# Expert lists of a routed MLP: odd experts filled from the other end, the eleventh weight chunk in two halves, the first two freed places refilled in quarters

## The reference

```python
g_prob = softmax(hf @ w_route_group + b_route_group)           # 4 groups, the best one is taken
e_logits = (hf @ w_route_expert + b_route_expert)[..., group]  # 8 experts in it, the best two are taken
comb = g_w * softmax(top_l)
out[token] += silu(x @ w_gate[e]) * (x @ w_up[e]) @ w_down[e] * comb     # for both experts e of each token
```

## Time and profile before

| | |
|---|---|
| median of 3 runs | 1010.31 us (1009.67 to 1010.51) |
| the profiled execution's own time | 1011.65 us |
| its span (first to last instruction) | 1009.7 us |
| mean granted TensorE clock | 0.965 |
| moved by DMA | 258.53 MB |

### The profile page before, as it was taken

The page is one execution under the profiler, slowest core; times in us unless marked ns, Lnnn a source line. Parts: engine busy times, 40 slices in busy tenths (PEclk is TensorE's granted clock), DMA queues, the critical chain, the costliest instruction groups (busy, mean ns, idle before and its releaser), DMA issues.

```text
span 1009.7 us, 11128 instructions
## 1 busy us (share of the span) xinstructions
PE 881.6 (87%) x4299; PEld 484.0 (48%) x4299; DVE 374.1 (37%) x827; ACT 218.3 (22%) x559; POOL 94.2 (9%) x104
## 2 busy tenths in 40 slices
PE   6999999999999999999799997768787777777674
PEld 4555777777688888654443332222222222222221
DVE  4589687786353445522742111011111110111110
ACT  3432645446332100121111111001010110101010
POOL 0100000000000000011011220101010101111011
PEclk9999999999999999999879999999898999899998
DMA  9621321121122227298389999999999999999991
GB/s 319 208 84 67 101 83 51 43 84 42 42 84 84 84 111 275 80 422 340 128 296 393 387 392 387 400 401 404 396 399 404 408 395 408 405 409 405 404 380 37
DMA packets 34916, 258.53 MB, mean 256 GB/s; under 512 B 9304, under 2 KB 12632, under 8 KB 19608
## 3 DMA queue, kind: packets, MB, share of 16 engines
q1 hardware_dynamic: 27904, 242.17, 60.6%
q0 software_dynamic: 6960, 15.65, 5.5%
HBM read 252.45 MB, written 14.58 MB: 264 GB/s over the span
## 4 chain that ended last, share of the span: by engine, by line
PE 77%; issue 7%; DMA 7%; DVE 4%; another core or an unknown queue 2%; ACT 1%; SPq 1%; POOL 0%; POOLq 0%; DVEq 0%; ACTq 0%
PE ps L1785 24%; PE ps L2069 20%; PE ps L2092 12%; PE ps L1723 6%; PE ps L1944 5%; DMA arena<-in_w_gu 5%; DMA arena<-in_x 2%; PE ps L2054 1%; PE ps L1870 1%; PE ps L1844 1%; PE ps L1801 1%; PE ps L1827 1%; PE ps L1978 1%; PE ps L2077 1%
## 5 line engine op out<-in xcount | busy, mean ns | idle before, releaser
L1785 PE MATMUL ps<-arena 128*128 128x272 f32 x1120 | 266.7, 394 | 2.7 <-DVE arena L1283 1.0
L2069 PE MATMUL ps<-arena 128*64 128x512 f32 x512 | 234.8, 606 | 30.7 <-DMA arena<-in_w_gu 30.2
L2070 PE MATMUL ps<-arena 128*64 128x512 f32 x512 | 235.2, 606 | 0.0
L1785 PEld LDWEIGHTS ps<-arena 128*128 128x128 f32 x1120 | 208.9, 190 | 52.3 <-issue 7.0
L753 ACT ACTIVATE arena<-ps 128x272 f32<-128x272 f32 (+4 forms) x156 | 71.4, 465 | 364.6 <-PE ps L2092 177.5
L2069 PEld LDWEIGHTS ps<-arena 128*64 128x64 f32 x512 | 66.7, 138 | 169.3 <-issue 130.7
L1578 DVE SCALAR_TENSOR_TENSOR arena<-arena,list_w,ps 64x512 f32<-64x512 f32 x32 | 24.0, 749 | 279.7 <-ACT arena L1010 279.7
L2092 PE MATMUL ps<-arena 128*64 128x512 f32 x256 | 67.6, 675 | 33.6 <-issue 32.7
L2092 PE MATMUL ps<-arena,const 128*64 128x512 f32 x256 | 68.1, 680 | 28.0 <-issue 27.6
L714 POOL DMA_INDIRECT out_y<-arena,list_i x32 | 45.7, 1427 | 399.9 <-DVE arena L1585 393.9
L1723 PE MATMUL ps<-arena 128*128 128x512 f32 (+1 forms) x192 | 75.5, 552 | 7.7 <-DVE arena L1076 7.7
(11 more groups left out here) (240 smaller groups left out, 714.6 us busy)
## 6 DMA issues: line engine op xcount, KB each, us to landing
arena<-in_w_gu SPq DMA_DIRECT2D x63, 2048.0 KB, 54.7
arena<-in_w_ed SPq DMA_DIRECT2D x31, 2048.0 KB, 54.9
arena<-in_w_pair SPq DMA_DIRECT2D x20, 1024.0 KB, 4.9
arena<-in_w_q SPq DMA_DIRECT2D x2, 2048.0 KB, 15.4
arena<-in_w_out SPq DMA_DIRECT2D x2, 2048.0 KB, 12.2
arena<-in_x SPq DMA_DIRECT2D x4, 512.0 KB, 10.5
arena<-in_w_gu SPq DMA_DIRECT2D x4, 512.0 KB, 44.6
arena<-in_w_ed SPq DMA_DIRECT2D x4, 512.0 KB, 28.6
```

The costliest lines, as they stand in the source:

```text
L1785: ins = mm(out, w[:, k, :], tokens[:, k, :], start=k == 0 and q in "127", stop=k == 3, skip_group_check=q not in "127")
L2069: mm(ps[0:C, 2 + s, :], xT[s][:, j, :], w[:, jj, 1, :], start=j == 0, stop=j == JX - 1)
L2070: ins = mm(ps[64:64 + C, 2 + s, :], xT[s][:, j, :], w[:, jj, 0, :], start=j == 0, stop=j == JX - 1)
```

## The change

Three things are changed.

**The lists.** A sign (`side`) is +1 for even experts and -1 for odd ones. For an odd expert the place counts down from 63 instead of up from 0. `choice` makes signed copies of the one-hot rows (`side_hot`, two operations more for each tile), `one_hot_bf` is their sum, and `tile_ranks` starts its sum with a product of one row, `first_place` (0 for even experts, 63 for odd ones). `count` takes the sign off again, and `list_items` has three operations more. The gathers, the additions and the number of rows of each stay as they are: only the places of the rows change. An even expert with 34 rows fills places 0 to 33, an odd one 30 to 63.

**The eleventh chunk** (number 10). Its first half is issued straight behind the two writes, its second half where the whole chunk was.

**The first two freed places.** Chunks 11 and 12 are issued in four pieces of 512 KB each. A piece waits only for the step of expert 0's gate and up that read the same quarter of the place.

```diff
+        def in_pieces(n):
+            return N_CHUNK <= n < N_CHUNK + 2
...
-            sp.wait_ge(x_full[0], 16)
-            load_chunk(EARLY + 2)
+            sp.dma_start(rows[:, 0:2], source[:, 0:2]).then_inc(chunk_in[N_CHUNK - 1], 16)
+            sp.wait_ge(x_full[0], 16)
+            sp.dma_start(rows[:, 2:4], source[:, 2:4]).then_inc(chunk_in[N_CHUNK - 1], 16)
...
+                if in_pieces(n):
+                    for q in range(PIECES):
+                        if q < PIECES - 1:
+                            sp.wait_ge(first_pieces, part * (PIECES - 1) + q + 1)
+                        else:
+                            sp.wait_ge((ga_used, gu_ready)[part], 1)
+                        rows, source = piece(n, q)
+                        sp.dma_start(rows, source).then_inc(chunk_in[n % N_CHUNK], 16)
+                    continue
...
+                ts(first_place[:], cc("side")[0:1, :], -0.5 * (C - 1), 0.5 * (C - 1), ALU.mult, ALU.add)
...
-                link(ts(hots[0], e_t, b1, None, ALU.is_equal))
+                ts(hots[0], e_t, b1, None, ALU.is_equal)
+                side = split(cc("side"), (EG, NG)).rearrange("p e g -> p g e")[0:r]
+                sided = [side_hot[0:r, c, :].rearrange("p (e g) -> p g e", g=NG) for c in range(2)]
+                link(stt(sided[0], e_t, b1, side, ALU.is_equal, ALU.mult))
...
-                link(ts(hots[1], e_t, b2, None, ALU.is_equal))
+                ts(hots[1], e_t, b2, None, ALU.is_equal)
+                link(stt(sided[1], e_t, b2, side, ALU.is_equal, ALU.mult))
...
-                tt(one_hot_bf[0:r, t, :], pick[0:r, 0, t, 1, :], pick[0:r, 1, t, 1, :], ALU.add).then_inc(choice_ready, 1)
+                tt(one_hot_bf[0:r, t, :], side_hot[0:r, 0, :], side_hot[0:r, 1, :], ALU.add).then_inc(choice_ready, 1)
...
-            link(dve.tensor_copy(count[:], ps[:, 7, 256:256 + NE]))
+            link(tt(count[:], ps[:, 7, 256:256 + NE], cc("side"), ALU.mult))
...
+                link(tt(tmp, sel, across(cc("side"), NOV), ALU.mult))
+                link(dve.tensor_reduce(steps, tmp, AX_X, ALU.add))
+                link(tt(item[:, 1, :], item[:, 1, :], steps, ALU.mult))
...
+                mm(ps[0:ROWS[t], 7, t * NE:(t + 1) * NE], ones_bf[0:1, 0:ROWS[t]], first_place[:], start=True, stop=False)
...
+                        if isinstance(e, int) and e == 0 and jj < PIECES - 1:
+                            ins.then_inc(first_pieces, 1)
```

More of the change, by code:

```diff
@@ L66 @@
                   ("inv_count", 4 * 16), ("group_rank", NG), ("expert_rank", NE),
-                  ("expert_id", NE), ("token", NT), ("place", C), ("chunk_edge", 8), ("item", NOV), ("before", P), ("band", 2 * P)):
+                  ("expert_id", NE), ("token", NT), ("place", C), ("chunk_edge", 8), ("item", NOV), ("side", NE), ("before", P), ("band", 2 * P)):
     CONST[_name] = (_at, _n)
@@ L107, in constants @@
     put("item", np.arange(NOV))
+    put("side", 1 - 2 * (np.arange(NE) % 2))
     q, k = np.arange(P)[:, None], np.arange(P)[None, :]
@@ L239, in build @@
         one_hot_bf = sb("one_hot_bf", [P, NT, NE], BF16)
+        side_hot = a_stat[:].rearrange("p s c v -> p s (c v)")
+        first_place = sb("first_place", [1, NE], BF16)
         count = sb("count", [P, NE])
@@ L530, in w_down, with piece @@
             return area(CHUNK_AT[n % N_CHUNK], JH, D)
+        PIECES = 4
+        def in_pieces(n):
+            return N_CHUNK <= n < N_CHUNK + 2
         def chunk_landed(n):
-            return 16 * (n // N_CHUNK + 1)
+            if n % N_CHUNK == N_CHUNK - 1:
+                return 16 * (n // N_CHUNK + 2)
+            return 16 * (n // N_CHUNK + 1) + (16 * (PIECES - 1) if n >= N_CHUNK and in_pieces(n % N_CHUNK + N_CHUNK) else 0)
+        def piece(n, q):
+            rows = area(CHUNK_AT[n % N_CHUNK], PIECES, 4096 // PIECES)[:, q]
+            part, e = chunk_of[n]
+            if part < 2:
+                return rows, a["w_gu"][expert_at(e), part][:, q].rearrange("p u n -> p (u n)")
+            return rows, a["w_ed"][expert_at(e)][:, q]
         block = ctx.enter_context(nc.Block())
@@ L625, in _ @@
             sp.dma_start(half_cols(o["y"], LAST), x_half(LAST)).then_inc(last_written, 16)
+            part, e = chunk_of[N_CHUNK - 1]
+            rows = (w_up if part < 2 else w_down)(N_CHUNK - 1)
+            source = a["w_gu"][expert_at(e), part] if part < 2 else a["w_ed"][expert_at(e)]
+            sp.dma_start(rows[:, 0:2], source[:, 0:2]).then_inc(chunk_in[N_CHUNK - 1], 16)
             sp.wait_ge(x_full[0], 16)
-            load_chunk(EARLY + 2)
+            sp.dma_start(rows[:, 2:4], source[:, 2:4]).then_inc(chunk_in[N_CHUNK - 1], 16)
             for n in range(N_CHUNK, 3 * NE):
                 part, e = chunk_of[n - N_CHUNK]
+                if in_pieces(n):
[7 more added lines that the diff above has]
+                    continue
                 sp.wait_ge((ga_used, gu_ready, dn_ready)[part], e + 1)
@@ L2062, in gate_up @@
                     if not pieces:
-                        pe.wait_ge(chunk_in[(n + h) % N_CHUNK], chunk_landed(n + h) + more)
+                        pe.wait_ge(chunk_in[(n + h) % N_CHUNK], chunk_landed(n + h) + more[h])
                     w = w_up(n + h)
@@ L2111, in _ @@
             filled = -(-3 * NE // N_CHUNK)
+            assert not in_pieces(2 + N_CHUNK)
             pe.wait_ge(item_ready, 1)
@@ L2118, in _ @@
                     turn_x(i + NE, 0, i * 16 + 16 * (NE // 2 + 1))
-                    gate_up(i + NE, 0, 0, i * 16 + 16 * filled)
+                    gate_up(i + NE, 0, 0, [i * 16 + 16 * (filled + PIECES - 1)] * 2)
                     turn_hid(i + NE, 0)
```

7 lines of the change are left out of this document (4 added, 3 removed).

## The result

| | before | after |
|---|---|---|
| median | 1010.41 us (1009.67 to 1012.06, 4 runs) | 999.5 us (996.93 to 1000.29, 4 runs) |
| ratio | | 0.9878, 95% interval 0.9864 to 0.9892 |
| the profiled execution | 1011.65 us, span 1009.7 | 996.93 us, span 995.0 |

By the ratio, which is used throughout, the change gains 12.3 us of 1010.4 (10.9 to 13.7), where 8.2 were forecast. The quotient of the two medians is 0.9892, 10.9 us, at the low end of that. The profiled execution of the changed kernel is the fastest of its four, so its profile shows still more gain, 14.7 us.

The account below looks back on a forecast made before the run. From about 520 us the 16 DMA engines were taken as the bound. 7.0 + 1.2 = 8.2 us off the profiled 1011.65 gives 1003.45, and the runs' median 1.34 us lower gives 1002.1 us; range 999.5 to 1007.5.

Parts of the forecast that it names:

- The longer table of constants is 16 KB.: Start of the kernel: the added constants were listed among covered costs, with no time charged.
- part 1: End of the weight stream: turning odd lists upside down evens the DMA engines' loads, -7.0 us.
- part 2: Start of the DMA-bound stretch: half chunk and quarters fill idle time, less the routing's delay, -1.2 us.
- place r goes to engine r modulo 16: Gathers and additions: assumed mapping, giving engine 0 81 filled places against a mean of 68.
- The 1.03 of the earlier trace: Last addition, 35 rows: DMA share in its first microsecond, read as all sixteen engines working, supporting modulo 16.
- The 29 us of the prediction: Part 1's saving if each engine took four neighbouring places: 104 rows at 0.28 us.
- The routing costs 1.5 us.: choice(1) to choice(4): eight VectorE operations 1.1 us, four TensorE products 0.4 us, delaying the first gather and chunk 13.
- Pieces of 512 KB are no slower than chunks where they follow each other.: Quarters of chunks 11 and 12: full rate expected, from 395 GB/s at share 0.98 in the last chunks' pieces.
- The queue runs empty, and chunk 13 takes 7.4 us.: After chunk 12's last piece: a new gap ahead of chunk 13, which lands 7.4 us after issue, at 534.9.
- places don't matter: Rival, end of weights: engines slow for another reason, part 1 between 0 and 3 us, middle 1008; chance 14%.
- four neighbouring places: Rival, row transfers: each engine takes four neighbouring places, so the time is 980 us; chance 1%.
- The slower case: Odd experts' rows on other partitions cost more through what they meet; 1015.5 us at 0.10 more a row; chance 4%.

Follow-up runs that it names:

- the start alone: Kernel before with half of chunk 10 ahead of the wait and chunks 11 and 12 in quarters, lists, constants and routing as before: 1010.63 us, ratio 0.9993.
- the lists alone: Kernel before with only the upside-down odd lists, SP's old order of whole chunks kept: 1000.81 us, ratio 0.989.
- the run without the half: Changed kernel with chunk 10 issued whole, no half ahead of the first gather, quarters kept: 1003.39 us, ratio 0.992.
- The staggered lists: Changed kernel, three versions with lists running upwards: odd lists from place 8, lists from 0, 8, 4, 12 in turn, odd lists from 16 (the last 1007.64 us).
- the run with all lists from place 0: Changed kernel with sign +1 for all experts, so odd lists start at place 0 as before: 1007.73 us, ratio 0.9965.

## Where the prediction held, and which step failed

**The step that failed** is among the edits costed at nothing: "The longer table of constants is 16 KB." The bytes are indeed hidden. But the table lies ahead of the arena, and its 128 bytes a partition moved the arena from 8448 to 8576, which made the mean weight packet of the stretch shorter by some 3 to 5 ns. That is 2 to 4 us, the difference between the 8.6 and 9.4 us that the change gives at a multiple of 256 and the 11.5 and 12.3 at an odd multiple of 128.

No row of the profile before could price this, since all of it ran at one place. The profile after had the sign of it: 403 against 399 GB/s at the same share of 1.01 over the whole stretch is no idle time filled at its start or its end.

**The forecast came out at the old place, partly by luck.** 1002.1 us had been forecast, and the changed kernel with the arena at 8448 took 1002.62. In its profile the unevenness gave 6.9 us (10.5 to 3.6), close to the 7.0 of part 1. The bulk gave another 1.8 us that the forecast did not have (450.0 to 448.3), and chunk 13 landed no earlier than before (mean 534.9 against 534.8), where part 2 had wanted 1.2.

**Part 1 (-7.0 us): the mechanism held, two of its terms were wrong and made up for each other.** The sixteen engines did end unevenly because every list starts at place 0, and turning every second list evened them. But "place r goes to engine r modulo 16" is wrong: with two neighbouring places to an engine the fullest has 27 places over the mean, 54 rows and not 26. And a row costs it 0.16 us at the end, not 0.28 to 0.45. The 1.03 of the earlier trace rows could not tell the mappings apart, because a window counts a packet's whole time where the packet begins:

```profile
1002.30:1002.50 0.20, 0.00 (x0) 0.00 (x0) 0.00 (x0) 0.00 (x0) 0.00 (x0) 1.00 3.21 307
```

Sixteen of the 35 rows begin within 0.21 us there. That speaks for sixteen engines at work, by pairs as well as modulo 16.

The Trainium skill, DMA: Bandwidth & Descriptors, section The descriptor swizzle, gives an engine two runs of four neighbouring partitions, 32 apart, in a transfer to 128 of them. In the indirect transfers to 64 here the counts fit two runs of two, 32 apart, and runs of four are excluded by the skipped places. By that section's formula as it stands, places 0 to 63 would be the work of eight engines, and my estimate from it, at the prediction's 0.28 us a row, is some 25 us for part 1 (44 places, 88 rows). The 29 us of the prediction belong to another mapping, four neighbours on each of sixteen engines.

**Part 2 (-1.2 us): neither shown nor refuted, and not by the way forecast.** The start alone gives 0.7 us (-0.4 to 1.8), and the changed kernel is ahead of the lists alone by 0.9878 / 0.989, 1.2 us, with intervals that overlap. Three steps can be checked.

- *The routing costs 1.5 us.* It costs 0.75. From the issue of the output weights (373.98 before, 372.88 after) to the issue of the last write to the output (495.44, 495.09) it is 121.4 to 121.5 us in all eight kernels with the old routing and 122.2 in all nine with the new one. In the three kernels that have TensorE's product and not the signed copies it is 121.6. So the product costs 0.1 us, where 0.4 had been forecast, and the eight operations 0.6 us, where it was 1.1.
- *Pieces of 512 KB are no slower than chunks where they follow each other.* At the end this is so, and in the run without the half from 520 us on. In the changed kernel from 514 to 522 us they ran at 310 GB/s. Their packets of 4 KB take 159 ns in the median here as at the end, but here 58 of 601 took over 300 ns, and the mean was 201 (160 at the end). Four of them make 802 ns, against the 611 of one packet of 16 KB. The gathers beside them are not the reason: only 5 gathered rows moved in these 8 us, and from 524 to 526, with 31 gathered rows, the pieces' packets took 162 ns in the mean. In the run without the half 806 of 807 packets from 520 to 528 took under 170 ns. What differs is the queue: here the pieces are carried as SP issues them, from 512.30 to 519.63, with little ahead of them. That this is the cause is argued and was not tested.
- *The queue runs empty, and chunk 13 takes 7.4 us.* In the changed kernel no gap came, since the slow pieces lasted until it was issued, and it took 9.3 us. In the run without the half the gap came and it took 7.5 us, and with the start alone 7.8 us.

**The rivals.** That places don't matter is refuted by the unevenness, four neighbouring places by the skipped places. The slower case (rows on other partitions raise the price of what they meet) did not come with the change: at 8448 the mean packet became 3 ns shorter (642.1 to 639.3). The staggered lists show that there is such a price: their mean packet is 2.1 to 4.6 ns longer than in the run with all lists from place 0, which is 1.4 to 3.2 us over 688 packets.

## What to carry to other kernels

When 16 DMA engines are the bound, count what each of them carries: rows that always fill a buffer from place 0 load the same engines each time, and filling every second one from the other end cures it for a few small operations. Take the mapping from the records of a skipped or short transfer before counting by it: a count with the wrong mapping can still give the right size once, as here. An added constant or small tensor ahead of a large buffer also moves the buffer: before a gain or a loss of half a per cent is put down to an edit, run the kernel before with the same shift and nothing else. Where transfers fill nearly all the time, try the buffer's beginning at both kinds of place; it costs one unused tensor.

## What the runs showed of the hardware that was not expected

- **Where the landing buffer begins changes the rate by nearly 1%.** In the kernel before, beginnings at 8320 and 8576 (odd multiples of 128 bytes) gave a median of 611 ns for a packet of 16 KB and 402 to 403 GB/s. Beginnings at 8192, 8448 and 8512 gave 613 to 615 ns and 399 GB/s. All chunks lie at multiples of 512 bytes within the arena, so they share its remainder. Why an odd multiple of 128 should be better is not shown; five beginnings were tried. The Trainium skill, DMA: Bandwidth & Descriptors, section How a descriptor splits into AXI transactions, says that a descriptor that does not start 256B-aligned pays for extra beats. It says so of the bytes that are fetched. If it held for the destination as well, the multiples of 256 would be the fast ones; the measurements have it the other way round.
- **An indirect transfer of up to 64 rows gives an engine two neighbouring places, and starts over at place 32.** This is inferred from counts, as the records name no engine: 44 rows left six engines with four rows and ten with two. A row more or less on the fullest engine costs 0.16 us at the end (48 rows, 7.5 us).
- **A high DMA share is not a high rate.** From 504 to 536 us a share of 0.87 moved 312 GB/s and a share of 0.83 moved 313. From 514 to 522 it was 0.95 with 310 GB/s, from 522 to 524 in the run without the half 1.03 with 420, with packets of 4 KB in both.
